# Seven half-size products for the output and gate projections of two layers, with weight sums on GpSimd

## The reference, cut to what matters

```python
y = mixed @ w_out                                    # 512x1024 @ 1024x1024
h = h + rms_norm(y, norm_post[layer])
gate = sigmoid(h @ ple_w_gate[layer])                # 512x1024 @ 1024x1024
h = h + (p[layer] @ ple_w_proj[layer]) * gate        # 512x256 @ 256x1024
```

## Time and profile before

| | |
|---|---|
| median of 3 runs | 2112.95 us (2110.01 to 2113.03) |
| the profiled execution: its time | 2112.67 us |
| its span, first to last instruction | 2110.3 us |
| PE busy | 1978.5 us (94%) |
| DVE, ACT, POOL busy | 645.1, 383.2, 265.6 us |
| DMA traffic | 486.59 MB, 231 GB/s on average |

### The profile page before, as it was taken

The page is one execution under the profiler, slowest core; times in us unless marked ns, Lnnn a source line. Parts: engine busy times, 40 slices in busy tenths (PEclk is TensorE's granted clock), DMA queues, the critical chain, the costliest instruction groups (busy, mean ns, idle before and its releaser), DMA issues.

```text
span 2110.3 us, 20503 instructions
## 1 busy us (share of the span) xinstructions
PE 1978.5 (94%) x8248; PEld 997.4 (47%) x8248; DVE 645.1 (31%) x1403; ACT 383.2 (18%) x782; POOL 265.6 (13%) x367
## 2 busy tenths in 40 slices
PE   8999999999999999999996998979898899979896
PEld 4688854444655544545543534324343434324333
DVE  2355542342898323143435101001020202001012
ACT  1033331114655111102311010100000010100002
POOL 3432100002687000001110000000000000000000
PEclk9999999999999999999997999999999999999998
DMA  9022240202111502412233799999999999999995
GB/s 267 3 61 60 81 150 0 80 11 89 60 41 64 190 1 100 122 39 69 91 120 159 316 426 429 425 428 429 427 428 427 427 427 427 427 429 426 428 427 213
DMA packets 100140, 486.59 MB, mean 231 GB/s; under 512 B 5855, under 2 KB 50234, under 8 KB 75984
## 3 DMA queue, kind: packets, MB, share of 16 engines
q1 hardware_dynamic: 97376, 480.79, 56.6%
q0 software_dynamic: 2384, 4.39, 0.7%
q10 hardware_dynamic: 288, 0.11, 0.0%
HBM read 483.13 MB, written 2.34 MB: 230 GB/s over the span
## 4 chain that ended last, share of the span: by engine, by line
PE 80%; DMA 12%; DVE 5%; ACT 2%; issue 1%; ACTq 0%; POOL 0%; POOLq 0%; DVEq 0%
PE bank L908 14%; PE bank L1412 13%; DMA arena<-in_w_up 12%; PE bank L900 12%; PE bank L1443 10%; PE bank L990 6%; PE bank L1363 3%; PE bank L1281 3%; PE bank L1389 2%; PE bank L930 2%; PE bank L1014 2%; PE bank L1433 2%; PE bank L1167 1%; PE bank L890 1%; PE bank L1236 1%; PE bank L1032 1%
## 5 line engine op out<-in xcount | busy, mean ns | idle before, releaser
L1412 PE MATMUL bank<-arena 128*64 128x512 f32 x2048 | 467.1, 614 | 68.7 <-DMA arena<-in_w_up 68.5
L1412 PEld LDWEIGHTS bank<-arena 128*64 128x64 f32 x2048 | 160.6, 142 | 372.2 <-issue 372.0
L908 PE MATMUL bank<-arena 128*128 128x512 f32 x704 | 306.6, 595 | 5.1 <-issue 4.3
L900 PE MATMUL bank<-arena 128*128 128x512 f32 x672 | 295.0, 597 | 0.0
L1443 PE MATMUL bank<-arena 128*64 128x512 f32 x960 | 218.7, 615 | 0.0
L908 PEld LDWEIGHTS bank<-arena 128*128 128x128 f32 x704 | 133.3, 191 | 169.2 <-issue 168.0
L900 PEld LDWEIGHTS bank<-arena 128*128 128x128 f32 x672 | 126.9, 191 | 154.6 <-issue 154.5
L2475 DVE TENSOR_TENSOR arena<-arena,bank 128x512 f32<-128x512 f32 x64 | 42.1, 685 | 408.7 <-PE bank L1389 408.1
L1498 ACT ACTIVATE arena<-bank 128x512 f32<-128x512 f32 (+3 forms) x130 | 70.4, 547 | 477.4 <-PE bank L908 147.0
L2490 DVE TENSOR_TENSOR arena<-bank,arena 64x512 f32<-64x512 f32 x64 | 44.5, 695 | 364.1 <-ACT arena L1737 362.5
L1737 ACT ACTIVATE arena<-bank 64x512 f32<-64x512 f32 x64 | 37.7, 589 | 551.4 <-PE bank L1412 509.4
(11 more groups left out here) (302 smaller groups left out, 1834.2 us busy)
## 6 DMA issues: line engine op xcount, KB each, us to landing
arena<-in_w_gate SPq DMA_DIRECT2D x64, 2048.0 KB, 23.7
arena<-in_w_up SPq DMA_DIRECT2D x64, 2048.0 KB, 27.1
arena<-in_w_down SPq DMA_DIRECT2D x60, 2048.0 KB, 23.2
arena<-in_att_w_in SPq DMA_DIRECT2D x24, 512.0 KB, 7.3
arena<-in_rec_w_in SPq DMA_DIRECT2D x12, 1024.0 KB, 5.7
arena<-in_ple_w_gate SPq DMA_DIRECT2D x4, 2048.0 KB, 11.6
arena<-in_w_down SPq DMA_DIRECT2D x8, 1024.0 KB, 16.7
arena<-in_w_in SPq DMA_DIRECT2D x6, 1024.0 KB, 8.3
```

Of the source, the lines that this page charges most:

```text
L900: mm = pe.matmul(bank[:, :], w[:, k, c:c + P], xT[:, k, :], start=(k == 0), stop=(k == KT - 1))
L908: mm = pe.matmul(bank[:, 0:n], xT[:, k, P * i:P * i + P], w[:, k, c:c + n], start=(k == 0), stop=(k == kt - 1))
L1412: mm = pe.matmul(banks[f][64 * part:64 * part + 64, :], xe[:, k, CAP * (e % 2):CAP * (e % 2) + CAP], w[:, kk, 512 * f:512 * f + 512], star ...
```

## The change

1. **Products.** In each tail the output and the gate projection are computed by the seven-product scheme. The contraction is cut in two (the first four and the last four blocks of 128 channels), the tokens in two (tiles 0 and 1 are "early", 2 and 3 "late"), the output columns in two. A product is four matmuls of 128x512 for each of two token tiles: 56 matmuls for a projection in place of 64. The p rows and all transposes stay.
2. **Weight sums.** POOL makes four sums of 128x2048 for each projection (`row_weight`), and also the four of `input_rows` that DVE made (`input_weight`). They stand on POOL's queue between the tile roots.
3. **Token sums and rows.** DVE makes four sums of 128x1024 of the transposed tokens for each projection (`token_sums`) and adds each product from its bank to rows in SBUF (`y`). ACT takes squares and sigmoid from these rows, 1024 columns at a time. The gain step reads SBUF too.
4. **Order.** PE now does products 1, 2, 6, 5, 3, 7 of the output projection for tiles 0 and 1, turns tile 0, product 4, turns tile 1, and so on (below). The gates come at the end of the tail.
5. **Slabs.** The slabs after both tails are placed and ordered anew. The first slab of the third layer's input weights (`hy`, 2 MB) is now issued only when DVE has finished all of `H` in layer 1.
6. **Recurrence.** DVE does three levels of the exponents before the states, not four (two for the first head); the rest follows after the states.

The diff, cut to its core (the first `tail` is POOL's, the second PE's; `post` is DVE's):

```diff
-        slab(("hy", 0), w_cols(wi, 0, 512), KT, 512, 8192, ("out", 1, 3, 1))
+        slab(("hy", 0), w_cols(wi, 0, 512), KT, 512, 4096, 2 * TT)
...
-                if after is not None:
+                if isinstance(after, int):
+                    sp.wait_ge(h_done, after)
+                elif after is not None:
                     sp.wait_ge(filled, nth(after))
...
+            def tail(layer):
...
+                row_weight("out", layer, 1)
+                row_weight("out", layer, 4)
+                row_weight("gate", layer, 3)
+                tile_root(0)
+                tile_root(1)
+                row_weight("gate", layer, 2)
+                tile_root(2)
+                tile_root(3)
+                row_weight("gate", layer, 4)
+                row_weight("gate", layer, 1)
+                input_weights(1)
+                tile_root(4)
+                tile_root(5)
+                input_weights(2)
+                tile_root(6)
+                tile_root(7)
+                input_weights(4, 3)
...
             def tail(layer, follow, last_ready, middle=None):
...
+                pair("out", 1)
+                pe.wait_ge(*last_ready)
+                for p in (2, 6, 5, 3, 7):
+                    pair("out", p)
+                for i in range(2):
+                    turned(i)
+                    product("out", 4, i)
+                for i in range(2):
+                    tile_done(("h", layer), i)
+                    product("gate", 1, i)
+                for i in range(2):
+                    product("gate", 2, i)
+                    turned(2 + i)
+                for i in range(2):
+                    tile_done(("h", layer), 2 + i)
+                    product("gate", 4, i)
+                pair("gate", 6)
+                pair("gate", 5)
+                if middle is not None:
+                    middle()
+                pair("gate", 3)
+                ple(0)
+                ple(1)
+                pair("gate", 7)
+                for i in range(2):
+                    ple(2 + i)
+                    pre(layer + 1, i, u_rows[i])
...
                 def post(i):
                     dve.wait_ge(y_squared, 4 * layer + i + 1)
-                    r = tile_root(i, tile_ss[:, 2 * i:2 * i + 1], tile_ss[:, 2 * i + 1:2 * i + 2])
+                    r = tile_root(i, tile_ss[:, 2 * i:2 * i + 1], None)
                     dve.wait_ge(dma_row, 16 * (layer + 1))
+                    step(dve.scalar_tensor_tensor(rows_[:, i, :], rows_[:, i, :], r, row[:, :], ALU.mult, ALU.mult))
+                    dve.tensor_tensor(H[:, i, :], H[:, i, :], rows_[:, i, :], ALU.add).then_inc(h_mixed, 1)
...
-                    exponents(h + 2, range(4))
+                    exponents(h + 2, range(2 if h == 0 else 3))
                 head_states(h)
...
-                    exponents(h + 2, range(4, 5))
+                    exponents(h + 2, range(2 if h == 0 else 3, 5))
```

More of the change, by code:

```diff
@@ L175, in row_ending, with row_joint, turned, ple @@
             yield from row_part("i1", p)
+    def row_joint(tag, layer, p):
+        for t in range(2):
+            yield (tag, layer, p, t), ("act" if p == 1 or (tag == "gate" and p == 4) else "dve")
     def tail(layer, follow, middle=()):
-        def out(i):
-            yield from rows(("out", layer, i), "dve", "dve")
-        for i in range(2):
[L182 to L192, removed]
+        def turned(i):
+            yield from rows(("h", layer, i), "act", "dve")
+        def ple(i):
+            yield from rows(("ple", layer, i), "dve", "dve")
+        for p in (1, 2, 6, 5, 3, 7):
+            yield from row_joint("out", layer, p)
+        out, gate = list(row_joint("out", layer, 4)), list(row_joint("gate", layer, 2))
+        yield from turned(0)
+        yield out[0]
+        yield from turned(1)
+        yield out[1]
+        yield from row_joint("gate", layer, 1)
+        yield gate[0]
+        yield from turned(2)
+        yield gate[1]
+        yield from turned(3)
+        for p in (4, 6, 5):
+            yield from row_joint("gate", layer, p)
+        yield from middle
+        yield from row_joint("gate", layer, 3)
+        yield from ple(0)
+        yield from ple(1)
+        yield from row_joint("gate", layer, 7)
+        for i in range(2):
+            yield from ple(2 + i)
+            yield from pre(layer + 1, i)
         if layer == 0:
@@ L820, in _ @@
             load_p(1)
-            tail_roots()
+            for n in (3, 2):
+                row_weight("out", 1, n)
+            tail(1)
             pool.wait_ge(filled, nth(("ple", 1, 3, 1)))
@@ L940, in tail, with pair, turned, ple @@
+                def pair(tag, p):
+                    product(tag, p, 0)
+                    product(tag, p, 1)
+                def turned(i):
                     pe.wait_ge(h_mixed, 4 * layer + i + 1)
                     tile_transposes(("h", layer), i, H[:, i, :])
[L942 to L947, removed]
+                def ple(i):
@@ L1474, in y_squares @@
                     act.wait_ge(*ready)
[L1475 to L1479, removed]
+                act.wait_ge(*drained(("out", layer, 3, i) if i < 2 else ("out", layer, 4, i - 2)))
+                act.activation(junk, y[layer][:, i, :], ACT.Square, scale=1.0 / 32.0, accum_out=tile_ss[:, 2 * i:2 * i + 1]
+                               ).then_inc(y_squared, 1)
                 junk_free[:] = [(y_squared, 4 * layer + i + 1)]
@@ L1528, in tail @@
             def tail(layer):
+                rows = y[layer]
                 def gates(i):
[L1530 to L1533, removed]
+                    act.wait_ge(*drained(("gate", layer, 3, i) if i < 2 else ("gate", layer, 7, i - 2)))
+                    act.activation(rows[:, i, :], rows[:, i, :], ACT.Sigmoid).then_inc(gates_ready, 1)
                 done = lambda i: (h_done, 4 * layer + i + 1)
+                for t in range(2):
+                    copy(rows[:, t, 512:D], ("out", layer, 1, t))
                 y_squares(layer, 0)
@@ new lines, in tail @@
+                for t in range(2):
+                    out_product(2, t)
+                token_sums("out", mixT[layer], (4,))
+                for p in (6, 5, 3):
+                    for t in range(2):
+                        out_product(p, t)
+                for t in range(2):
+                    post(t)
+                    out_product(7, t)
+                for t in range(2):
+                    transposed(("h", layer), t, 1, hT2, None)
+                    out_product(4, t)
+                for t in range(2):
+                    post(2 + t)
+                    gate_product(2, t)
+                    transposed(("h", layer), 2 + t, 1, hT2, None)
@@ L1998, in tail @@
+                dve.wait_ge(*drained(("h", layer, 3, 0)))
+                dve.wait_ge(*drained(("h", layer, 3, 1)))
+                token_sums("gate", hT2, (1, 3, 2, 4))
+                for t in range(2):
+                    gate_product(6, t)
+                for t in range(2):
+                    gate_partial(t)
+                for t in range(2):
+                    gate_product(5, t)
                 if middle is not None:
                     middle()
-                transposed(("h", layer), 2, 1, hT2, None)
```

326 lines of the change are left out of this document (224 added, 102 removed).

## The result

The changed kernel takes 2123.9 us in the median of 20 runs (2115.2 to 2129.0), the kernel before 2113.0 (2109.4 to 2119.0). The ratio is 1.0043, 95% interval 1.0029 to 1.0057: slower by about 9 us. The runs of the changed kernel stand in three bunches, near 2115.5, 2124 and 2128. Those of the kernel before stand in two: 15 of the 20 between 2109.4 and 2114.4, five between 2117.8 and 2119.0, and no profile caught one of these five. The changed kernel's profile is of a run of 2115.59 us (span 2113.8), which is 2.9 above the profiled execution of before, so the trace of the changed kernel shows only about a third of the loss.

A forecast was written before the change was run, and what follows sets the result against it. The prediction took PE as the bound, busy 94% of the span and almost alone in both tails' chains. Its terms, −27.5 − 4.3 + 33.3 + 1 = +2.5 us, gave 2115.5 us against a median of 2112.95; range 2090 to 2123.

The forecast's parts named there:

- my three cases: Total against the kernel before: faster 0.36, same (within 0.2%) 0.26, slower 0.38.
- Products: Both tails, PE: four projections lose eight matmuls each at 0.858 us, −27.5 us.
- old waits: Both tails: PE's four existing waits for DVE go with their order, −4.3 us.
- POOL's sum: Weight sums in the tails: 2048 columns take 4.5 us, extended from rows of 256 and 512 columns.
- The hold: Tails: a DVE operation on two SBUF operands waits until POOL's ends; seen to 1.28 us, extended to sums of 4.5.
- rival A: Tails: the hold is short, waits about 8 to 11 us with collisions, total 2092 us; chance 0.27.
- New waits: PE waits for DVE at turns of tiles 1 and 3 and tail ends: 17.4 us layer 0, 15.9 layer 1, +33.3.
- The slab: After layer 1's tail: later issue of `hy` costs nothing, or 1 to 2 us if the cover is gone.
- Recurrence: Heads: one level of exponents moves behind the states; nearest no change, taken as +1 us.
- Rival B: Heads: the moved level delays ACT, each of six heads grows by 1 us, +6, total 2121.5; chance 0.18.

The follow-up runs named there:

- sums_moved: The changed kernel with three gate sums and the second input sum at other places of POOL's queue; 2091.6 us, ratio 0.9892 to the kernel before.
- sums_late: sums_moved with input-row sums 2, 4 and 3 delayed until DVE has scaled the last tile's rows; 2090.1 us, ratio 0.9879 to the kernel before.
- GpSimd's pieces: The changed kernel with each of POOL's weight sums in the tails cut into four of 512 columns; 2108.4 us, ratio 0.9969 to the kernel before.

## Why the prediction was right

The forecast was 2115.5 us, +2.5 to the kernel before, with a range of 2090 to 2123. Measured are a median of 2123.9 in the first 20 runs, just above that range, 2116.3 in the 12 later ones, and 2115.6 in the profiled execution. So the way of the change and the holds were right, and its size was not: about 9 us by the ratio of the first runs and 4 by that of the later ones. Slower was the likeliest of my three cases, but by little, 0.38 to 0.36 for faster. Point by point:

- **Products, −27.5, and old waits, −4.3.** Right. 80 records took 34.35 to 34.54 us, 0.86 a matmul as before. The kernel without sums shows the whole saving at work, −24 us with the waits that remain.
- **POOL's sum, 4.5 us from a line through two rows.** Measured 4.50 and 4.51. Two took 5.5, which is the hold the other way. In the changed kernel DVE's token sum of 1.2 us was itself held by the sum ahead, got in behind it and ran until 318.40; POOL's next sum, from 317.27, was longer by as much. POOL, then DVE:

```profile
312.80 4.51 POOL L764 TENSOR_TENSOR arena<-arena 128x2048 f32<-128x2048 f32 x1 [2.35 <-PE bank L1042]
317.27 5.50 POOL L745 TENSOR_TENSOR arena<-arena 128x2048 f32<-128x2048 f32 x1
```

```profile
312.83 0.69 DVE L2110 TENSOR_TENSOR arena<-bank,arena 128x512 f32<-128x512 f32 x1 [0.70 <-PE bank L1042]
313.44 4.96 DVE L2127 TENSOR_TENSOR arena<-arena 128x1024 f32<-128x1024 f32 x1
```

The first of DVE's two rows is the other half of the prediction's reading: an operation on a bank and one SBUF row, beside a sum of 4.5 us, takes its 0.69 us and isn't held.

- **The hold.** The extension from 1.28 us to 4.5 held: DVE's step of 0.22 us took 4.49. The rule of the Trainium skill (SBUF — State Buffer, "SBUF: two separate sides") that the lock is kept for the whole instruction is borne out to 4.5 us by the changed kernel's own trace. The 2092 of rival A is near what the kernel without sums does, 2089.0.
- **New waits, 33.3.** At the turn of tile 1 3.34 measured for 3.0, at that of tile 3 9.73 for 9.9, the end of layer 0 3.1 for 4.5, of layer 1 2.5 for 3.0: 31.7 in all. In the end of layer 0, I had put the wait at the turn of scaled tile 2; it stands before the first input product, which waits for DVE's gain step on the turned rows of scaled tile 0.
- **The slab, 0.** Right: PE's use at 871.54 follows its work without a pause.
- **Recurrence, +1.** Measured −0.4 by itself. Rival B was wrong: the heads didn't grow longer (233.5 to 236.7 us for 236.9). I had put PE's wait for the states at 0.72 us a head at most, from a row of one head; the first head's is 3.30 us. The edit took it away, and PE's new waits for ACT took nearly as much back.
- **The missing term.** By my terms with the measured waits, layer 0's tail would be 181.8 − 13.7 − 2.3 + 16.2 = 182.0; it is 186.8 and 189.4 in the two profiles. Layer 1's would be 150.7 − 13.7 − 2.0 + 15.6 = 150.6; it is 152.4 and 153.9. The 6.6 and 10.7 us that are missing are half clock behind the waits, but for 0.6 us of one more wait in the second profile. "PE waits 9.9 us" was priced at 9.9, and that was the step that failed: a wait of PE cost its length and then 0 to 3 us of slow work behind it, differently from run to run. That 2115.6 looked like a hit is partly luck, for the kernel before had lost 3 us to half clock in its heads, which the changed kernel did not in that run.

What stays open: the bunch at 2128 us and the upper bunch of the kernel before, which no profile caught, why the same wait is followed by half clock in one run and not in another, and the half clock between 100 and 150 us that two profiles have (granted 0.90 in sums_moved and sums_late, 1.00 in the seven others), which costs 5.8 us there (304.6 for 298.8). PE stands idle there for 1.7 us in every profile. The work up to there is the same as in the changed kernel; whether the two edits have a part in it isn't shown. PE's windows of sums_late:

```profile
100.00:150.00 50.00, 48.30 (x207) 0.90 0.26 64
```

## What to carry to other kernels

Before work moves to GpSimd because it is idle, look at what VectorE does in the same microseconds. In these traces an operation of VectorE with two or more operands in SBUF waited until the end of the GpSimd sum beside it, even an operation on a single column; one with one SBUF operand and a bank or constants didn't. The same 20 sums cost 26 us and more behind the roots (2115.5 in the lowest bunch against 2089.0 without them), and 1 us in better places of the same queue (2090.1). And a new wait of the bottleneck engine can be worth more than its length: price what its clock does behind it, and judge such a change by many runs.

## What was not expected of the hardware

- TensorE's clock at half behind a wait of 3.34 us in one run and at full behind the same wait in another (348.29 and 347.84), which is a part of the spread of one kernel's times over 2115 to 2129 us. Filling the waits with matmuls of no use made the tails 2.3 and 1.6 us shorter, not longer.
- A VectorE operation with a constant and one SBUF operand of one column (`L1973`, 0.15 us) ran beside one of GpSimd's pieces without a hold, while its neighbours with two operands or more each paid 0.8 to 1.0 us.
